# A four-quadrant layout for a chunked recurrence, with its step reordered, and weight remainders placed behind the squares of the norms

## The reference, cut to what matters

```
def rmsnorm(x, g):
    y = x * lax.rsqrt(jnp.mean(x * x, axis=-1, keepdims=True) + NORM_EPS)
    return y * g

def step(S, inp):                      # 8 heads, S is 64 x 64 per head, 768 tokens, both directions
    r_t, w_t, k_t, v_t, a_t, b_t = inp
    sa = jnp.einsum('bhij,bhj->bhi', S, a_t)
    S = (S * w_t[:, :, None, :] + sa[..., None] * b_t[:, :, None, :]
         + v_t[..., None] * k_t[:, :, None, :])
    return S, jnp.einsum('bhij,bhj->bhi', S, r_t)
```

## Time and profile before

| what | us |
|---|---|
| median of 3 executions | 2980.38 |
| lowest of the three | 2979.22 |
| highest of the three | 4762.29 |
| the profiled execution | 2992.32 |
| its span (first to last instruction) | 2990.5 |

### The profile page before, as it was taken

One profiled execution on the slowest core, in us unless ns is written; L12 is line 12 of the kernel. 1 busy time (PEld: TensorE's weight loads), 2 busy tenths in 40 slices (PEclk: granted clock), 3 DMA queues, 4 the chain that ended last, 5 costly groups with the idle time before them and its releaser, 6 DMA issues.

```text
span 2990.5 us, 55539 instructions
## 1 busy us (share of the span) xinstructions
PE 2587.5 (87%) x23248; PEld 2003.5 (67%) x23248; DVE 1742.7 (58%) x2676; ACT 1190.3 (40%) x1728; POOL 407.4 (14%) x447
## 2 busy tenths in 40 slices
PE   6979889999986889988888888889995879988995
PEld 5745467878764556865777757677775646766774
DVE  3655545444443554436677773489985265547996
ACT  2423333222232146233222222457764247545774
POOL 1010000000011020002434310212211030011221
PEclk9978979999998789996999989899997989989998
DMA  4247812222210000100000031189984200026996
GB/s 168 85 161 277 328 57 97 86 84 85 103 67 32 6 1 1 71 22 2 4 4 4 4 128 62 46 314 417 402 335 185 80 1 2 15 76 262 412 415 247
DMA packets 63819, 385.05 MB, mean 129 GB/s; under 512 B 7840, under 2 KB 7856, under 8 KB 27232
## 3 DMA queue, kind: packets, MB, share of 16 engines
q1 hardware_dynamic: 41792, 292.60, 25.5%
q0 software_dynamic: 21792, 89.08, 7.7%
HBM read 344.91 MB, written 36.70 MB: 128 GB/s over the span
## 4 chain that ended last, share of the span: by engine, by line
PE 72%; DVE 10%; DVEq 5%; ACT 3%; issue 3%; DMA 3%; POOL 1%; PEld 1%; PEldq 1%; ACTq 1%; POOLq 0%; SPq 0%
PE psum L427 14%; PE psum L631 12%; PE psum L3037 9%; PE psum L2121 4%; PE psum L1171 4%; PE psum L3059 4%; PE psum L1190 3%; PE psum L1181 2%; PE psum L1811 2%; PE psum L2683 2%; PE psum L1717 2%; PE psum L409 2%; DMA weight_slots<-in_weights 2%; DVEq L2302 1%; PE psum L1029 1%
## 5 line engine op out<-in xcount | busy, mean ns | idle before, releaser
L427 PE MATMUL psum<-arena_r 128*128 128x512 f32 (+1 forms) x976 | 312.4, 361 | 4.3 <-DVE weight_slots_r L453 4.2
L631 PE MATMUL psum<-arena_r 128*128 128x512 f32 x704 | 250.8, 397 | 10.8 <-issue 3.9
L427 PE MATMUL psum<-arena_r,weight_slots_r 128*128 128x512 f32 (+1 forms) x696 | 249.0, 358 | 0.0
L448 ACT ACTIVATE arena_r<-weight_slots 128x1024 fp32r<-128x1024 f32 x73 | 76.5, 1058 | 335.3 <-PE psum L427 251.0
L2121 PE MATMUL psum<-x_t 64*64 64x64 f32 x5376 | 181.8, 221 | 31.9 <-DVEq L2302 15.0
L631 PE MATMUL psum<-arena_r,weight_slots_r 128*128 128x512 f32 x528 | 209.1, 396 | 0.0
L427 PEld LDWEIGHTS psum<-arena_r 128*128 128x128 f32 x976 | 179.2, 190 | 35.7 <-issue 4.3
L2121 PEld LDWEIGHTS psum<-x_t 64*64 64x64 f32 x5376 | 167.7, 135 | 43.8 <-DVEq L2302 19.8
L427 PE MATMUL psum<-h_t_r,arena_r 128*128 128x512 f32 (+1 forms) x528 | 192.3, 364 | 0.0
L3007 DVE TENSOR_TENSOR weight_slots_r<-weight_slots,arena_r 128x2048 fp32r<-128x2048 f32 x78 | 177.8, 2287 | 12.3 <-ACT arena_r L3002 11.8
L3007 DVE TENSOR_TENSOR weight_slots_r<-weight_slots,h_t_r 128x2048 fp32r<-128x2048 f32 x72 | 164.1, 2286 | 15.1 <-ACT h_t_r L3002 14.7
(11 more groups left out here) (456 smaller groups left out, 5531.3 us busy)
## 6 DMA issues: line engine op xcount, KB each, us to landing
weight_slots<-in_weights SPq DMA_DIRECT2D x277, 1024.0 KB, 7.1
y_rows<-arena POOLq DMA_DIRECT2D x50, 512.0 KB, 7.8
h_rows<-arena POOLq DMA_DIRECT2D x10, 512.0 KB, 2.9
x_keep<-x_t POOLq DMA_DIRECT2D x1, 3072.0 KB, 9.0
x_t<-x_keep POOLq DMA_DIRECT2D x1, 3072.0 KB, 14.8
x_t<-in_x POOLq DMA_DIRECT2D x1, 2048.0 KB, 9.8
out_x<-x_t SPq DMA_DIRECT2D x1, 2048.0 KB, 7.2
arena<-in_toe POOLq DMA_DIRECT2D x1, 1792.0 KB, 7.1
```

The lines of the kernel that those rows point to most:

```text
L427: last = self.nc.tensor.matmul(self.bank(n), w[:, kt, :], self.operand(part, kt, a, b), start=(i == 0), stop=(i == len(passes) - 1))
L448: self.nc.scalar.activation(self.w_hi[:, t % 2], self.tile_weights(self.kern.slots, t), ACT.Copy).then_inc(self.rounded[0], 1)
L631: last = nc.tensor.matmul(bank, w(p, k), x(q, k), start=(k == j == 0), stop=(k == n - 1 and j == 2))
```

## The change

1. **Levels joined, four quadrants.** The two halves g are gone: each product of a level is one group of 16 matmuls, each copy and each addition one instruction of 512 columns. A new placing (`home`, `plain`, `turned`) puts a unit's matrices so that `half` and `grow` read one half of the partitions and write the other for every second pair. Their order (`units`) goes round the four quadrants. `grow_turned` reads and writes the same half, so it stays at two.
2. **Step order.** The grams of the next step are issued behind level 4 instead of at the next step's start. The product with the state moves up to level 1, that with the keys to levels 2 and 3, the outputs' share of the state to level 4. ACT weighs the keys (four ACTIVATEs, in place of DVE's L2257). Identity blocks are preset by POOL and overwritten under a mask (`copy_predicated`), in place of DVE's mask-and-add. A sixth gram (`turned_gram`) gives the transposed product.
3. **State and outputs.** DVE adds the state, signals it, adds the outputs, and only then multiplies the state by its decay.
4. **Norms.** `first_rest` stands behind the squares, and only for the first weight item; the second item's rounding and remainder are the new `more_rounded` and `more_rest`, at the end of the norm (rounding still early where `early` is on). For the plain projections both tiles remain in `first_rounded` and `first_rest`. The norm ahead of the output projection of block one gets `early=False`.

```diff
 class Norm, before_scalar / vector / scalar:
-    def before_vector(self, dve):
-        if self.ahead is not None and self.early:
-            self.ahead.first_rest(dve)
+            self.ahead.more_rounded(act)
...
         for t in self.by_vector:
             ...
+        if self.ahead is not None and self.early:
+            self.ahead.first_rest(dve)
         n = 32 * len(self.blocks)
         dve.wait_ge(self.roots[0], self.roots[1] + 1)
...
+        if self.ahead is not None:
+            self.ahead.more_rest(dve)
 class Experts (MoeFront alike, with rest_item):
     def first_rest(self, dve):
-        for j in (0, 1):
-            self.rest_half(dve, 0, j, 0)
-            self.rest_half(dve, 0, j, 1)
+        self.rest_half(dve, 0, 0, 0)
+        self.rest_half(dve, 0, 0, 1)
+
+    def more_rest(self, dve):
+        self.rest_half(dve, 0, 1, 0)
+        self.rest_half(dve, 0, 1, 1)
 class Wkv:
+    def home(c, d):
+        return d ^ (c % 2)
+    def plain(self, x, c, e, d):
+        at = c // 2 * 256 + self.home(c, d) * P + e * 64
+        return x[64 * d:64 * d + 64, at:at + 64]
+    def turned(self, x, c, e, d):
+        r, at = 64 * self.home(c, d), c // 2 * 256 + d * P + e * 64
+        return x[r:r + 64, at:at + 64]
+        units = [(2 * a + (d ^ r), e, d) for a in (0, 1) for e in (0, 1) for d, r in corners]
...
             for lv in range(self.LEVELS):
-                half(lv, 0)
-                half(lv, 1)
-                whole(lv, 0)
-                whole(lv, 1)
+                half(lv)
                 if lv == 0:
-                    gram(4, 0)
-                    gram(4, 1).then_inc(self.sem("last_grams"), 1)
-                if lv == self.LEVELS - 2:
-                    from_state()
-                    from_keys()
+                    pe.wait_ge(*self.at("token_rows", n, 2))
+                    gram(n, 4).then_inc(self.sem("last_grams"), 1)
+                if lv == 1:
+                    w_from_state()
+                if lv == 2:
+                    w_from_keys(0)
+                if lv == 3:
+                    w_from_keys(1)
+                if lv == last_lv:
+                    y_from_state()
+                ready(lv)
+                if lv < last_lv:
+                    grow(lv)
+                grow_turned(lv)
+            if n + 1 < self.STEPS:
+                first_grams(n + 1)
...
 DVE, at the end of a step:
+            if more:
+                low(n + 1)
+                new_keys(n + 1)
+                up(n + 1)
+            state(n)
+            outputs(n)
+            decayed(n)
 block one:
-        out_norm = Norm(self, h, mixed_all, KT, 2, segs, lambda t, a: c("out_norm", t), parts=mixed_lat)
+        out_norm = Norm(self, h, mixed_all, KT, 2, segs, lambda t, a: c("out_norm", t), parts=mixed_lat, early=False)
```

More of the change, by code:

```diff
@@ new lines, in tensor, with bank_of, operands, gram @@
+        last_lv = self.LEVELS - 1
+        units = [(2 * a + (d ^ r), e, d) for a in (0, 1) for e in (0, 1) for d, r in corners]
+        def bank_of(first, r, c, e, out):
+            at = c // 2 * P + e * 64
+            return psum[64 * out:64 * out + 64, first + r, at:at + 64]
+        def operands(n):
+            at, rt = w.at[n % 2], w.rt[n % 2]
+            return (w.bt, at), (at, w.bt), (w.kt, at), (w.bt, rt), (w.kt, rt)
+        def gram(n, i):
+            lhs, rhs = operands(n)[i]
+            first, off = self.GRAMS[i]
+            for c in range(4):
+                for e, d in corners:
+                    at = off + c // 2 * P + self.home(c, d) * 64
+                    last = t.matmul(psum[64 * d:64 * d + 64, first + e, at:at + 64], self.by_dim(lhs, c, d, e),
+                                    self.by_dim(rhs, c, d, e), start=True, stop=True)
+            return last
@@ new lines, in turned_gram, with turn @@
+        def turned_gram(n):
+            first, off = self.TURNED_GRAM
+            for c in range(4):
+                for e, d in corners:
+                    r, at = 64 * self.home(c, d), off + c // 2 * P + d * 64
+                    last = t.matmul(psum[r:r + 64, first + e, at:at + 64], self.by_dim(w.bt, c, d, e),
+                                    self.by_dim(w.at[n % 2], c, d, e), start=True, stop=True)
+            return last
+        def turn(bank, x):
+            for c in range(4):
+                last = t.transpose(psum[:, bank, c * P:(c + 1) * P], x[:, c * P:(c + 1) * P], ident)
+            last.then_inc(self.sem("tokens"), 1)
@@ new lines, in step @@
+                if lv == 3:
[8 more added lines that the diff above has]
+                first_grams(n + 1)
+            pe.wait_ge(*self.at("level_added", n, self.sum_of(last_lv, 1)))
+            for c, e, d in units:
+                last = t.matmul(bank_of(6, self.home(c, d), c, e, d), self.turned(w.xt, c, e, d), self.turned(w.wv, c, e, d),
+                                start=True, stop=True)
@@ L2197, in step @@
+            pe.wait_ge(*self.at("u_copied", n))
+            for c in range(4):
+                for e, d in corners:
+                    last = t.matmul(s_of(c, e, d), self.token_rows(w.br, c, e, d), self.plain(w.uv, c, e, d), start=False, stop=(c == 3))
             last.then_inc(self.sem("state_summed"), 1)
@@ new lines, in step @@
+                if lv == 1 and more:
+                    growths(n + 1)
+                if lv == 2 and more:
+                    scaled(n + 1, 0, 1, 2, 3)
+                if lv == 3:
+                    act.wait_ge(*self.at("w_summed", n, 2))
+                    s.activation(self.four(w.wv), self.by_head(0, 0), ACT.Copy).then_inc(self.sem("w_copied"), 1)
+            act.wait_ge(*self.at("u_summed", n))
+            s.activation(self.two(w.uv), self.by_rows(6), ACT.Copy).then_inc(self.sem("u_copied"), 1)
@@ new lines, in mask, with low @@
+        def mask(i, dst, m):
+            return v.tensor_tensor(out=self.four(dst), in0=self.by_head(*self.GRAMS[i]), in1=spread(m), op=ALU.mult)
+        def low(n):
+            dve.wait_ge(*self.at("grams", n, 0))
+            dve.wait_ge(*self.at("grams", n, 1))
+            mask(0, w.lt, w.strict).then_inc(self.sem("masked"), 1)
+            dve.wait_ge(*self.at("presets", n, 0))
+            v.copy_predicated(out=self.four(w.x), mask=spread(w.first_low.bitcast(I32)),
+                              data=self.by_head(*self.GRAMS[1])).then_inc(self.sem("masked"), 1)
@@ L2312, in step, with up, state @@
+        def up(n):
+            dve.wait_ge(*self.at("grams", n, 2))
+            dve.wait_ge(*self.at("presets", n, 1))
+            v.copy_predicated(out=self.four(w.xt), mask=spread(w.first_up.bitcast(I32)),
+                              data=self.by_head(*self.TURNED_GRAM)).then_inc(self.sem("masked"), 1)
+        def state(n):
             dve.wait_ge(*self.at("state_summed", n))
             x = self.quads(w.s)
-            total = self.kern.psum[:, 4:6, 0:256].rearrange("p d (c t) -> p c d t", c=4)
```

390 lines of the change are left out of this document (205 added, 185 removed).

## The result

The changed kernel takes 2929.68 us (median of 4 runs, 2927.44 to 2938.82) where the kernel before takes 2979.8: a ratio of 0.9839, with a 95% interval from 0.9821 to 0.9856. That is 50 us or 1.6% less. The forecast was 2886, with a range from 2858 to 2925: the direction was right, the forecast gain is nearly twice the measured one, and the time lies above the range. The prediction gave 0.84 to a gain of more than 2% and 0.11 to a smaller difference, which is what came. The profiled execution took 2927.44 us.

A forecast was written before the change was run, and what follows sets the result against it. The recurrence was taken as close to PE-bound, with PE partly waiting for DVE. A step of 22.9 instead of 29.72 us gave 82 us, norms 12: 94 off 2992.3, so 2898, or 2886 as a median; range 2858 to 2925.

The forecast's parts named there:

- PE work of a step: Recurrence step: 21 four-quadrant groups, 7 two-quadrant groups and transposes, 10.5 + 7.1 + 1.4 = 19.0 us on PE.
- The rule of the Trainium skill: Matmul starts never under about 25 ns apart; four-quadrant groups then 0.80 us, 3.9 more per step, 2933 in all.
- Levels 0 to 3: First four levels of a recurrence step: 3.1 + 2.95 + 3.5 + 2.95 = 12.5 us.
- Level 4 to the next level 0: End of a recurrence step, from level 4's half to the next step's half, DVE setting the end: 10.2 us.
- 0.2 for small gaps: Last term of the recurrence step's sum, 12.5 + 10.2 + 0.2 = 22.9 us.
- Masked copies: DVE's 512-column copy_predicated from PSUM, two on the step's path: 0.69 us taken each, 0.6 to 1.38 possible.
- Decay: DVE's multiplication of the state, 0.69 us, stands behind y_added at the step's end and costs nothing.
- rival d: Recurrence: waits at step ends hold the clock at the 1.2 GHz level, 76 us more, 3044; chance 0.05.
- Norms: New order in the feed-forward, expert and other norms gains 12 us in sum, range 6 to 15.
- Rival (a): DVE bounds more of the recurrence (masked copies 1.38 or POOL collisions): step 26, 56 us gained, 2924; chance 0.15.

The follow-up runs named there:

- e2: Changed kernel with each group's first half sent to two quadrants in turn, the second half to the other two, same instructions: 2931.5 us.
- e6: Changed kernel with four units in a row sent to the same quadrant, same instructions: 2995.8 us, 1.0064 of the kernel before.
- e5: Changed kernel without two groups of products that only y uses, one dummy product in the place of each: 2922.0 us.
- e1: Kernel before with only the change's part on the norms, its recurrence kept: 2976.4 against 2981.7 us, ratio 0.9985.
- e9: Changed kernel's recurrence with the norms of the kernel before: 2943.7 us, 0.9863 of the kernel before.
- e8: Changed kernel with the kt-weighted grams joined, and also w and y products sharing weights (state, then v): 2899.8 us, 0.9741 of the kernel before.
- e4: Changed kernel with the two grams that have kt as weights joined into 16 products of 128 columns: 2915.2 us.

## Why the prediction was wrong

1. **PE work of a step** (forecast 19.0 us). Four-quadrant groups run at 15.6 ns a record, seven groups at two quadrants as before. Busy time is 255.3 / 12 = 21.3, by the profile's own count, which includes each group's end; the same count of mine was 1.4 short before the change (23.7 against 300.8 / 12 = 25.1) and is 2.3 short now. Right in mechanism. The rule of the Trainium skill (TensorE: Matmul & The Clock Gate, the section on 56 ns against 53.3 ns) that would make it 2933 is not followed here: starts are 15 to 16 ns apart.
2. **Levels 0 to 3** (forecast 3.1, 2.95, 3.5, 2.95). In the step shown 3.25, 3.48, 3.62 and 3.30: 13.65, with three stops of 1.74. Without them 11.9, against 12.5.
3. **Level 4 to the next level 0** (forecast 10.2). 14.89, with three stops of 3.84. Without them 11.05, of which the low clock made 1.1.
4. **"0.2 for small gaps."** This is the step of the prediction that failed: it put TensorE's time without instructions at nothing, and it measured 3.9 us a step. The sum of work and chain, 22.9, is what the kernel shows once the idle time is left out: (319.5 - 46.9) / 12 = 22.7. The idle time itself, 3.9 us a step, was no term of the sum. It appears because the forecast step takes a good quarter of the time between two packets away and the change adds three packets: 22.9 us a step would have wanted one every 12 x 22.9 / 84 = 3.3 us, and they come every 3.8 to 3.9. Taking the idle time off is a simplification, since other work can run into the stops (e2, e6); what shows the stops to be a cost of their own is e5, where the same work with fewer instructions took 17.5 us less.
5. **Masked copies** (0.69 taken, up to 1.38 feared): 0.72 to 0.75. **Decay**: free, but mis-sized, 0.69 to 1.15 and not 0.69. **Clock** (rival d): 0.99 over the stretch. It did fall once behind long stops, for 3.4 us, the thing that (d) feared; it cost about 1 us and not 76.
6. **Norms** (forecast 12): 5 by e1, 8 to 14 by e9, with local gains of 4 us in two of them as worked out. Right within what can be told. How much of the last norm's 4.2 us reaches the end can't be told: from its root to the end, the two profiles with the norms of before differ by 6 us already (342.9 in the kernel before, 349.0 in e9).
7. **Rival (a)** gives nearly the measured time (2924) and is nevertheless wrong: VectorE's operations between the grams and `y_added` cost what I took, and it waits for TensorE's stops. A right number from a wrong cause; e5, in which VectorE's work is unchanged, would have come out at no gain by it.

The hint was there before: six stops of up to 1.2 us with "issue" in a stage whose packets come every 4.46 us. I had looked at what TensorE waits for by engine, not at how many instructions a microsecond of the new step would need.

## What to carry to other kernels

Where a stage consists of thousands of small matmuls in straight-line code, count its instructions per microsecond before speeding up each one: in this kernel a packet of 256 came every 3.8 to 3.9 us on average where TensorE waited for them (single ones 3.3 to 4.5 apart), and a stretch that works off 256 in less gains little by faster matmuls. Stops named "issue" at equal distances in records are the sign, and joining products that share weights (more columns, fewer instructions) is then worth more than faster matmuls: e8 gained 30 us with TensorE equally busy. Before trusting one profile for a few microseconds, take a second one of the same kernel.

## What the runs showed of the hardware

- TensorE's instructions arrive 256 at a time (84 packets for 10757 matmul and 10749 weight-load records) and the arrival became the limit. From one packet's end to TensorE's going on it took 1.39 us, from there to the next packet's start 1.22, and the packet 1.08. The Trainium skill (Runtime: NRT & Kernel Launch, Instruction fetch mechanics) names refills of this size and holds them hidden behind the execution; here they were not: 46.9 and 54.9 us of stops.
- 64x64 matmuls, start to start per record, from the first to the last of a group (medians of the kept traces): 15.4 ns round four quadrants (`half` and `grow` of the changed kernel); 31.2 with two in turn (L2121 of the kernel before); 28.5 for `grow_turned`, which changes between two after every second unit; 24.5 in e2, which changes to the other two in the middle of a group; 41 to 43 for four units in a row in one quadrant (e6), and 48.3 for e6's `grow_turned`, which changes only twice in 16 units.
- TensorE's clock fell to 0.51 for 3.4 us behind stops of 1.37 and 1.91 us in one step of the changed kernel; stops of up to 1.65 us in its other steps left it at 1.00.
- With 128 columns (e4) a record takes 29 ns round four quadrants, so columns double and time nearly doubles.
- `copy_predicated` from PSUM, 128x512: 0.72 to 0.75 us, hardly more than an addition of that size (0.69).
